# Pair items of latent attention in another order, turned probabilities released bank by bank, context outputs over eight banks, and the first weight unit in quarters

## The reference

```
q = rms_norm(cq) @ w_uq            # 8 heads x (128 nope + 64 rope)
q = [rms_norm(q_nope) | axial_rotary(rms_norm(q_rope))]   # rotary for latents only
k_nope, v = rms_norm(ckv) @ w_ukv  # 8 heads x (128 + 128);  k_nope = rms_norm(k_nope)
k_rope = axial_rotary(rms_norm(k_rope))                   # one for all heads
latent queries attend to context and latent keys (768), context queries to context keys (256)
y = softmax(q k^T / sqrt(192)) v  @ w_o
```

## Time and profile before

| | |
|---|---|
| Median of the runs, lowest, highest | 3136.11, 3135.81, 3136.31 us |
| Profiled execution, its own time and its span | 3135.86 us, 3134.2 us |
| TensorE busy | 3019.6 us, 96% of the span |
| VectorE, ScalarE busy | 1811.6 us (58%), 859.2 us (27%) |
| Granted clock of TensorE, mean | 0.990 of full |

### The profile page before, as it was taken

How to read it: one execution, slowest core, us unless ns; L and a number is a source line. 1 busy time by engine, 2 the same in 40 slices (tenths; PEclk the granted TensorE clock), 3 DMA queues, 4 the chain that set the end, 5 groups by cost and what they waited for, 6 DMA issues and landing times.

```text
span 3134.2 us, 42265 instructions
## 1 busy us (share of the span) xinstructions
PE 3019.6 (96%) x17512; PEld 2624.0 (84%) x17512; DVE 1811.6 (58%) x2632; ACT 859.2 (27%) x1184; POOL 36.7 (1%) x73
## 2 busy tenths in 40 slices
PE   6999999999989899999999999999899999999999
PEld 4888888877877788888888888888788888888887
DVE  4675655765665676565674456566654646564454
ACT  3211111353454422111132112113322323242221
POOL 0000000000000000000000000000000000000000
PEclk8999999999999999999999999999899999999999
DMA  6332332111011143232321222232111212123222
GB/s 245 135 127 94 114 107 107 54 48 54 28 54 41 41 175 121 94 120 94 113 82 60 79 109 107 94 111 76 54 56 52 81 40 81 49 73 107 94 92 82
DMA packets 40984, 277.81 MB, mean 89 GB/s; under 512 B 4352, under 2 KB 5632, under 8 KB 8000
## 3 DMA queue, kind: packets, MB, share of 16 engines
q1 hardware_dynamic: 31024, 205.85, 18.2%
q0 software_dynamic: 9872, 70.72, 6.2%
HBM read 274.45 MB, written 2.10 MB: 88 GB/s over the span
## 4 chain that ended last, share of the span: by engine, by line
PE 88%; DVE 7%; ACT 2%; issue 2%; DMA 0%; SPq 0%; DVEq 0%; ACTq 0%
PE ps L311 28%; PE ps L313 28%; PE ps L312 28%; PE ps L630 2%; PE ps L339 1%; DVE wl L1303 1%; DVE act_buf L1387 1%; ACT wh L913 1%; DVE xnl L1391 1%; DVE irms L1594 0%; PE ps L325 0%; DVE ssum L1366 0%; DMA ada_w<-ada 0%; PE ps L357 0%; ACT xnh L944 0%
## 5 line engine op out<-in xcount | busy, mean ns | idle before, releaser
L311 PE MATMUL ps<-xnh,wl 128*128 128x512 f32 (+1 forms) x3040 | 1062.0, 349 | 28.4 <-DVE wl L1303 15.6
L312 PE MATMUL ps<-xnl,wh 128*128 128x512 f32 (+1 forms) x3040 | 1052.3, 346 | 0.0
L313 PE MATMUL ps<-xnh,wh 128*128 128x512 f32 (+1 forms) x3040 | 1050.8, 346 | 0.0
L311 PEld LDWEIGHTS ps<-xnh,wl 128*128 128x128 f32 x3040 | 580.2, 191 | 111.1 <-DVE wl L1303 17.4
L313 PEld LDWEIGHTS ps<-xnh,wh 128*128 128x128 f32 x3040 | 580.6, 191 | 70.3
L312 PEld LDWEIGHTS ps<-xnl,wh 128*128 128x128 f32 x3040 | 580.9, 191 | 67.9 <-issue 1.0
L1303 DVE TENSOR_TENSOR wl<-raw,wh 128x2048 fp32r<-128x2048 f32 (+2 forms) x183 | 402.3, 2199 | 142.0 <-ACT wh L913 141.7
L913 ACT ACTIVATE wh<-raw 128x2048 fp32r<-128x2048 f32 (+2 forms) x178 | 326.7, 1835 | 564.8 <-PE ps L313 564.8
L1445 DVE SCALAR_TENSOR_TENSOR h<-ps,coef,h 128x512 f32<-128x512 f32 x624 | 371.7, 644 | 105.4 <-PE ps L313 103.9
L311 PE MATMUL ps<-hidh,wl 128*128 128x512 f32 (+1 forms) x1232 | 422.2, 343 | 3.3 <-DVE h L1403 3.3
L313 PE MATMUL ps<-hidh,wh 128*128 128x512 f32 (+1 forms) x1232 | 423.2, 344 | 0.0
(11 more groups left out here) (240 smaller groups left out, 2987.9 us busy)
## 6 DMA issues: line engine op xcount, KB each, us to landing
raw<-weights SPq DMA_DIRECT2D x183, 1024.0 KB, 4.8
adaw<-ada POOLq DMA_DIRECT2D x64, 1024.0 KB, 5.1
ada_w<-ada SPq DMA_DIRECT2D x8, 1024.0 KB, 20.2
h<-x_in SPq DMA_DIRECT2D x1, 2048.0 KB, 8.8
c_act<-c_rows POOLq DMA_DIRECT2D x2, 1024.0 KB, 5.1
out<-h SPq DMA_DIRECT2D x8, 256.0 KB, 2.0
h<-x_in SPq DMA_DIRECT2D x1, 1024.0 KB, 27.8
cs<-rope_mla POOLq DMA_DIRECT2D x1, 512.0 KB, 3.4
```

What stands on the lines that cost most here:

```text
L311: mm(dst, lhs[1][rows], rhs[0][rows], start=first, stop=False)
L312: mm(dst, lhs[0][rows], rhs[1][rows], start=False, stop=False)
L313: return mm(dst, lhs[0][rows], rhs[0][rows], start=False, stop=last)
```

## The change

`spread` for the two-head rope item uses a matrix that holds both heads (`by_head`, loaded by GpSimd during the first pair), in one pass instead of two. Items live in rows of their own, the reciprocal has two buffers, ScalarE takes an item's two banks in one instruction. The order of the items is rope, query 0, key 0, query 1, key 1. The rope item is multiplied by its gain as ScalarE copies it, swapped and rotated at once, and scaled by its norm behind that. The tile order is context and latents of head 0, latents and context of head 1.

```diff
-W_BANKS = (1, 4, 2, 5)
-TILES = [(hh, q) for hh in range(2) for q in (4, 0, 1, 2, 3)]
+TILES = [(0, q) for q in (4, 0, 1, 2, 3)] + [(1, q) for q in (0, 1, 2, 3, 4)]
+C_BANKS = (2, 5, 6, 7, 1, 4, 0, 3)
+C_ORDER = (4, 6, 0, 7, 5, 1, 2, 3)
+E_BANKS = ((1, 0), (0, 0), (4, 0), (3, 0), (2, 0), (5, 0), (2, L), (5, L))
 # SP, start
-                if u in (1, 3):
-                    sp.dma_start(raw[:, u // 2, :], weights[u // 2]).then_inc(raw_full[u // 2], 16)
+                if u in (1, ADA_0 - 1):
+                    s = int(u > 1)
+                    sp.dma_start(raw[:, s, :], weights[s]).then_inc(raw_full[s], 16)
 # TensorE, start: step_of(k) waits for the quarter k // 2 of unit 0 and for activation k
+                    for g in range(KD // 2):
+                        if g + 1 < KD // 2:
+                            ada_sums(g + 1)
+                        step_of(2 * g)
+                        if g + 1 < KD // 2:
+                            ada_turn(g + 1)
+                        step_of(2 * g + 1)
+                    pe.wait_ge(w_ready[1], c.next(w_ready[1]))
+                    chain(1, 1, 4, 0, STREAMS[0])
                     norm_sums(1)
+                    chain(0, 1, 3, 0, STREAMS[0], ks=range(0, 4))
                     norm_spread(1)
+                    chain(0, 1, 3, 0, STREAMS[0], ks=range(4, KD))
                     first_ctx(0, 1)
 # TensorE, first_ups (all other feed-forwards); the retention's first head likewise
-                    chain(0, s1, 3, 0, parts[0])
+                    chain(0, s1, 3, 0, parts[0], ks=range(0, 4))
                     norm_spread(1, parts)
+                    chain(0, s1, 3, 0, parts[0], ks=range(4, KD))
 # TensorE, turn
                     for kc in range(6):
+                        if kc == 4 and n >= 1:
+                            pe.wait_ge(pt_ready, c.next(pt_ready))
 ...
+                        if kc in (3, 5):
+                            ins.then_inc(pt_full, 1)
 # TensorE, pair (not first)
+                    pe.wait_ge(q_part, c.next(q_part))
+                added()
                 project(0, lambda k: w(s0, k * 384 + 256), cq, 3)
+                    pe.wait_ge(w_ready[s0], c.next(w_ready[s0]))
+                added()
+                project(1, lambda k: w(s0, k * 384), cq, 3)
+                item_sum(1, L, item_sqs[0], mat=ones64)
+                turned_half(item_rows[0], 0)
+                added()
+                pe.wait_ge(w_ready[s1], c.next(w_ready[s1]))
+                project(2, lambda k: w(s1, k * 512), ckv, 2)
+                item_sum(3, L, item_sqs[1])
+                added()
+                item_spread(0, heads=True)
+                pe.wait_ge(item_rot, c.next(item_rot))
+                project(3, lambda k: w(s0, k * 384 + 128), cq, 3)
+                item_sum(5, L, item_sqs[0])
                 pe.wait_ge(item_v, c.next(item_v))
+                item_spread(1)
                 project(4, lambda k: w(s1, k * 512 + P), ckv, 2)
+                item_sum(1, L, item_sqs[1])
                 pe.wait_ge(item_v, c.next(item_v))
+                item_spread(0)
 ...
+                scores(0, *TILES[0])
                 pe.wait_ge(item_v, c.next(item_v))
+                item_spread(0)
+                scores(1, *TILES[1])
 # TensorE, tiles
+                    if n == 7:
+                        pe.wait_ge(o_ready, c.next(o_ready))
+                        weigh(1, 0)
+                    if n == 8:
+                        pe.wait_ge(w_ready[s0], c.next(w_ready[s0]))
+                        pe.wait_ge(o_ready, c.next(o_ready))
+                        pe.wait_ge(exp_done, c.next(exp_done))
+                        project_out(0, 0)
+                        project_out(2, 0)
+                weigh(1, 1)
+                pe.wait_ge(pt_ready, c.next(pt_ready, 2))
+                weigh(1, 2)
 # TensorE, context outputs of a pair that is not the last
+                    for m in range(KD):
+                        ins = project_ctx(m, 0, C_BANKS[m], 0)
+                    ins.then_inc(wo_used, 1)
+                    for m in C_ORDER:
+                        project_ctx(m, 1, C_BANKS[m], 0)
+                    return
 # ScalarE, pair
+            def take(n_item, between=None):
                 act.wait_ge(item_full, c.next(item_full))
+                fn(item_sqs[n_item % 2], both(n_item), ACT.Square)
+                if between is not None:
+                    root(*between)
+                if n_item:
+                    ins = fn(item_rows[n_item], both(n_item), ACT.Copy)
+                else:
+                    ins = fn(item_rows[n_item], both(n_item), ACT.Identity, scale=v("qg_rope"))
+                ins.then_inc(item_sq, 1)
 ...
+                take(0)
+                take(1)
                 root(ROPE, 1)
+                take(2, (NOPE, 3, L, 1, 1))
 # VectorE, pair: reciprocal, rotation, then the rope item's scaling
                 inverse()
+                rotated(item_rows[0], 0)
+                scaled(item_rows[0], None)
+                inverse(1)
 ...
+                    if n == 0:
+                        lo(kn[:, 1, 1, :], kn[:, 0, 1, :], item_rows[4])
 # VectorE, context outputs
+                for n, m in enumerate(C_ORDER):
+                    add_part(m, STREAMS[1], C_BANKS[m])
+                    if n == 1:
+                        dve.wait_ge(w_hi[s0], c.next(w_hi[s0]))
+                        for a, b, done in ((256, 384, q_part), (0, 256, w_ready[s0])):
+                            of = [t[:, s0, 0:Q_HI].rearrange("p (k e) -> p k e", k=3)[:, :, a:b] for t in (wl, raw, wh)]
+                            tt(of[0], of[1], of[2].bitcast(F32), ALU.subtract).then_inc(done, 1)
 # VectorE, end of the last pair: early_lo(s, q) splits a quarter of the next unit, before the activations
+                    inverse_rms(0, parts)
+                    add_part(0, parts[1], *E_BANKS[0], done=3)
+                    add_part(1, parts[1], *E_BANKS[1])
+                    for q in range(4):
+                        early_lo(early, q)
+                    normed(0, layer, k, parts)
```

More of the change, by code:

```diff
@@ L327, in quarter_sums, with spread @@
                 return ins
[L329 to L341, removed]
+            def spread(banks, inv, n_tok, heads=False):
+                n = n_tok // 4
+                for g in range(4):
+                    mat = quarter[:, 2 * g:2 * g + 1].to_broadcast([P, P]) if not heads else by_head[:, g, :]
+                    for bank, t0, t1 in ((banks[0], 0, S), (banks[1], S, T)):
+                        a, b = max(t0, g * n), min(t1, g * n + n)
+                        if a < b:
+                            ins = mm(ps[:, bank, a - t0:b - t0], mat, inv[:, a - g * n:b - g * n], start=True, stop=True)
                 return ins
@@ L377, in last_y, with ffn, chain @@
                 c.next(y_added, KD + 3)
-            def ffn(n_streams, slot, parts=STREAMS, start=False):
+            def ffn(n_streams, slot, parts=STREAMS, start=False, in_quarters=False):
                 streams = STREAMS[:n_streams]
-                def chain(half, s, bank, col, part, fresh=False):
+                def chain(half, s, bank, col, part, fresh=False, ks=range(KD)):
                     t0, n = part
-                    for k in range(KD):
+                    for k in ks:
                         if fresh:
@@ L548, in project, with item_sum, item_spread @@
                 ins.then_inc(item_full, 1)
-            def item_sum(bank, at=L, first=True, last=True, mat=ones, sq=sqb):
+            def item_sum(bank, at, sq, first=True, last=True, mat=ones):
                 pe.wait_ge(item_sq, c.next(item_sq))
                 quarter_sums(bank, at, sq, T, first, last, mat).then_inc(item_ms, 1)
-            def item_spread(halves=1):
+            def item_spread(buf=0, heads=False):
                 pe.wait_ge(item_inv, c.next(item_inv))
-                spread((6, 7), irms[:], T, halves).then_inc(item_rms, 1)
+                spread((6, 7), inv[buf], T, heads).then_inc(item_rms, 1)
             def w_in(s, j):
@@ L654, in pair, with added, turned_half @@
             def pair(first=False, last=False):
-                pe.wait_ge(w_ready[s0], c.next(w_ready[s0]))
                 cq = lambda k, t0, n: (cqn[:, 0, k, t0:t0 + n], cqn[:, 1, k, t0:t0 + n])
                 ckv = lambda k, t0, n: (ckvn[:, 0, k, t0:t0 + n], ckvn[:, 1, k, t0:t0 + n])
+                def added(n=2):
+                    if not first:
+                        pe.wait_ge(y_added, c.next(y_added, n))
+                def turned_half(rope, bank):
+                    mm(ps[:, bank, :], swap, rope[:, 0:S], start=True, stop=True).then_inc(item_swapped, 1)
@@ L819, in head @@
                         for k in range(KD):
+                            if first and not i and j and k == 4:
+                                norm_spread(1)
                             if first and i and j == 0:
@@ L1409, in add_pair @@
                 j = int(t0 == S)
```

(2 more changed lines are left out.)

452 lines of the change are left out of this document (230 added, 222 removed).

## The result

The changed kernel takes 3054.69 us (median of 4 runs, 3053.63 to 3057.61) against 3135.96 for the kernel before: the ratio is 0.9743, 95% interval 0.9728 to 0.9759. The profiled execution is the slowest of the four, 3057.61 us around a span of 3055.9, 78.3 us shorter than the span before.

A forecast was written before the change was run, and what follows sets the result against it. TensorE was taken as the bound, so its gaps were summed: start 13, norm's spread 9.5, pairs 35.8, into the feed-forward 2, less 3.4 for the clock: 57 us, giving 3079 us, range 3069 to 3100.

The forecast's parts named there:

- The second pair: Second pair of heads: 8.8 us shorter, from less idle time, a one-pass spread and no low clock.
- the rival theory: Stated for the follow-up runs: the pairs' additional gain has one large cause, the clock; no chance given.
- The 0.85 at the fourth turn: Wait in a pair's second half, 0.92 us before, forecast to stay as 0.85 because of VectorE's work.
- the 0.77 and 1.7: Gains per pair: 0.77 us from spreading two heads in one pass, 1.7 us from the low clock going.
- The start: Up to the first context product: 14.0 us earlier by the working, 13 taken, bounds 6 and 16.
- order of transfers: At the start: second weight unit behind all modulation units brings groups 2 and 3 forward by 2.5 us.
- Norm's spread: Context norm's spread moved into the middle of a chain: 3 x 2.7 plus 1.4, sum 9.5 us, bounds 5 and 10.
- Into the feed-forward: Feed-forward after the pairs: quarters split before the activations leave 2 us of gain, bounds 0 and 4.
- two falls of 1.7: Deduction of 3.4 us for two falls of the clock, at places the prediction couldn't name.
- Small waits instead of large ones: In the pairs, VectorE's fixed order brings new waits; half of the 36 us lost, 3097 us; chance 0.24.
- The slower case: In the pairs, five items become a bare serial chain with TensorE waiting at each: 3143 us; chance 0.03.
- The low clock once in each pair: Low clock comes in each pair in spite of all: 3082 us, held inside the forecast's 0.65.

The follow-up runs named there:

- Run 3: Changed kernel, but a tile's two turned banks are filled, copied and released together again: 3062.02 us.
- Run 4: Changed kernel, but the two output products between the ninth and tenth turn are done behind the tenth: 3059.93 us.
- run 8: Kernel before, with one edit of the change: turned banks filled, copied and released one by one: 3123.12 us.
- run 5: Changed kernel, but a pair's context outputs use four banks as before and the next pair's first projection waits for the whole split: 3057.95 us.
- run 9: Changed kernel, but the query's rope half is turned and rotated behind its norm again: 3063.02 us.
- run 7: Changed kernel, but the query's spread for two heads is done in two passes of 64 rows, as before: 3057.33 us.
- run 6: Changed kernel, but a pair's first projection waits for all 1152 weight columns instead of the third it reads; eight banks stay: 3054.28 us.
- run 10: Changed kernel with the old order of SP's transfers, second weight unit ahead of the modulation units of groups 2 and 3: 3055.65 us.
- run 1: Changed kernel, but the context norm's spread stands behind the whole chain of 24 matmuls again, in four places: 3063.51 us.
- run 11: Changed kernel plus a root on a dead tile behind each pair's last exponential but the last pair's, loading the root's table early: 3053.48 us.

## Why the prediction was wrong

Its direction and its mechanism held; the step that failed is the size of "The second pair: idle 8.9 -> 2.5, so 6.4; plus 0.77 and 1.7: 8.8", and with it the 35.8 us for the pairs. Measured: 12.70 in that pair, 53.4 in all. For a middle pair the difference of 3.9 us has two parts, up to rounding, and the clock, the rival theory's one cause, is not among them:

- **Idle time that I left in place, 1.7 us.** I kept 2.5 and 0.83 is there. The 0.85 at the fourth turn is the largest part: it did not come. I had added up VectorE's work there with the turned banks as one thing. Run 3 puts them together and a wait of 0.27 us comes at just this turn, so this explains about a third of the 0.85; the rest stays open. The wait behind the table load came as 0.65 instead of 1.0, the one for the rotation as 0.18 instead of 0.35, and the 0.3 for tight places did not come.
- **Busy time that I did not see as waiting, 2.1 us** (4.58 less the 0.77 and 1.7 that I had). I added the printed idle times. Where a stall follows, a matmul's row is fully counted as busy, though in the flow its end is overlapped: 0.25 us of a turn's row, 0.16 of a 256-column product's (0.28 long, 0.12 apart), 0.07 of a sum's. Run 4 shows it: 0.97 printed, 1.22 lost. The second pair before had eight such places, which by these sizes make 1.4 us; about 0.4 of it is left in the changed kernel. Also, a spread directly ahead of a sum took 1.62 us from start to start, ahead of a projection 1.39 (785.63 before, 754.48 after), and three spreads changed their place; that is 0.7 of the 2.1, and some 0.4 stays without a place. I took these from the two traces; apart from the turn's 0.25 no run isolates them.
- **The clock: nothing.** The low clock of a middle pair cost 1.7 us of work (0.39 x 4.43 in the second row below), as I had said. But it did not lengthen the pair by 1.7. From the ninth turn's start to the tenth's, in the first pair (full clock) and in the second (low clock) before:

```profile
741.54:745.23 3.69, 2.65 (x22) 2.48 (x22) 2.40 (x6) 1.31 (x4) 0.00 (x0) 1.00 0.00 0
839.47:843.90 4.43, 4.21 (x21) 3.98 (x22) 2.40 (x6) 1.31 (x4) 0.00 (x0) 0.61 0.00 0
```

The stretch is 0.74 us longer, since the wait behind it shrinks from 1.04 to 0.22 us. So 1.7 is right as a term beside the idle time of this pair, in which only the 0.22 stood, and it is not what a steady clock alone would have given.

In the last pair the clock fell twice, at 990.3 and at 1038, and cost 3.4 us of work instead of 1.7. From the first pair I took off 1 us for missing records; the amount was right for another reason, since the 12.1 us held 1.2 of the wait at the next pair's head and the pair's own idle time is 10.96. What the gain of a middle pair consists of, by the runs: release bank by bank 3.5 us in a pair of the kernel before (run 8), the work put between the last turns 1.2 (run 4), the eight banks 1.6 (run 5), rotation ahead 2.4 (run 9), the heads' spread in one pass 0.5 (run 7), the early third 0.3 (run 6), which is part of the 1.6. That makes 9.2 of 12.7. It is a rough sum, because it takes pieces from two kernels: in the changed kernel the release bank by bank is worth 1.7 (run 3). The rest, sums ahead of spreads with two reciprocal buffers and the new order of tiles, wasn't tried by itself.

The other steps. **The start**: the working gave 14.0 us at the first context product and 14.06 came. That it agrees so well is luck: the first step came 0.9 us later than in the working, the second unit 1.3 earlier (47.31 against 48.6), and what lies between it and the first context product took 1.3 longer. I then took 13 for a stretch of low clock. It came, at 23.0, and the two later stretches of before (at 41 and 75) went, so 15.7 us are kept. Its piece on the order of transfers was too large, 2.5 against 0.8 (run 10). **Norm's spread**: 9.5 forecast, 8.6 measured, 8.8 by run 1. **Into the feed-forward**: 1.3 of 2, the 2.99 us wait for VectorE's four quarters. **The clock**: two falls of 1.7 were taken off. The changed kernel's profile has five stretches of low clock (near 23, 999, 2163, 2671 and 2692), the one before thirteen, and each of the five has its like there, so none is a loss against it; what is left is the 0.68 us of rest, found at the start of the retention.

The rivals. Small waits instead of large ones, the chance that I had priced at 0.24, did not come: the range's upper half was spent on it, and the side below 3072 got 0.05. The slower case decides once four of five items are bare; none is. The low clock once in each pair did not come either: 1.00 in all four. The Trainium skill's "TensorE: Matmul & The Clock Gate" (psum-queue depth-cycling) tells of a bf16 kernel in which small idles between the banks let the clock swing. In runs 3 and 4 stalls of 0.26 to 1.06 us between the turned banks came back in every pair with the clock at 1.00, so it does not describe this kernel. And the drain that "ScalarE: Activation LUTs" (What ACT_TABLE_LOAD costs) adds to a load is not in these rows: the load at 745.65 takes 1.28 us and its ACTIVATE starts at 746.95, and taking it away gained 1.43 us (run 11).

## What to carry to other kernels

Size a stall from start to start: the next instruction's start less the last one's, less that one's pitch, which is the distance between the two starts where nothing waits. The printed idle time was up to 0.25 us short at a stall here, and with eight stalls in a repeated stage that is a term of its own. Where small stalls are removed from a bound engine, forecast what the stage would take with its own pitches alone, and argue only for the waits that must stay; I argued for those that might. The same holds for a low clock: where a stall follows, it hides a part of what the clock cost, here about half of 1.7 us. A split, a swap or a table load costs nothing in front of a wait that is there anyway, and moving one there can be worth more than the wait that it removes (run 9).

## What the runs showed of the hardware

The clock's falls are not the same in all executions of one program. The second group of modulation sums, the same 32 matmuls behind a short wait for their DMA, took 3.60 us in the changed kernel's profile and 1.93 in that of run 7:

```profile
22.66 1.93 PE L450 MATMUL ps<-ada_w,c_col 128*32 128x256 f32 x32 [1.00 <-DMA ada_w<-ada]
```

and behind the 2.99 us wait the steps ran at the low clock in the changed kernel's profile (0.77 us its first row) and at the full one in run 4's (0.47):

```profile
1000.14 0.77 PE L330 MATMUL ps<-xnh,wl 128*128 128x512 f32 x1 [2.99 <-DVE xnl L1460]
```

Run 4, the same instruction:

```profile
1003.44 0.47 PE L330 MATMUL ps<-xnh,wl 128*128 128x512 f32 x1 [2.99 <-DVE xnl L1460]
```

The first is worth 1.8 us: from these sums to the first pair's norm it is 623.39 us in the one and 621.56 in the other (646.39 and 644.22 by the clock of the trace; the other 0.3 is the first transfer, which landed later). The second is worth 1.8 us too: from this step to the feed-forward's first product with `hidh` that waits for `h` (1542.19) it is 542.05 us in the changed kernel and 540.28 in run 4. There is a third place, in the last feed-forward. The same instructions, in the changed kernel and in run 4:

```profile
2670.50:2700.67 30.17, 27.98 (x222) 26.50 (x222) 22.72 (x51) 13.44 (x32) 0.00 (x0) 0.89 0.21 71
```

```profile
2672.54:2700.39 27.85, 25.03 (x223) 23.50 (x223) 22.38 (x51) 13.44 (x32) 0.00 (x0) 1.00 0.22 76
```

That is 2.3 us; in the retention ahead of it run 4 loses 0.5 of them. The changed kernel's profile, the slowest of its four runs, has all three falls, run 5's has none of them. They are larger together than the 4 us between the changed kernel's fastest and slowest run, and they are why medians here can differ by a microsecond or two from what the traces' stretches say. From the first pair's norm to the next feed-forward, where none of them lies, runs 3 to 7 and 9 take 7.2, 5.1, 4.7, 0.7, 2.5 and 8.3 us more than the changed kernel; their medians say 7.3, 5.2, 3.3, -0.4, 2.6 and 8.3. That the falls are what sets the other runs' times apart was not shown, since only profiled executions have rows.

Within the pairs no profile of the changed kernel or of its eleven variants shows a low clock; the longest wait there is 1.62 us (run 9, at 925.87). In the pairs of the kernel before and of run 8 falls stand behind waits of 1.76 to 2.19 us, and not behind all of them.
